# SSD decay exponents from running sums, spread over partitions by DMA and raised on ScalarE, in a bidirectional SSD, S5 and FFN network

## The chip, the cores and the metric

One core of one Trainium2 chip runs the whole network as one program. The metric is the device time of that program in microseconds (us); lower is better.

## The reference, cut to what matters

Two layers on x (512 positions, 1024 channels, float32): an SSD mixer in layer 0 and an S5 mixer in layer 1, each followed by a convolutional FFN and a gated embedding. Only the SSD mixer is touched. It has 32 heads of 64 channels in 4 groups, two directions, and chunks of 128 positions:

```python
def ssd_chunked_scan(xh, dt, a, bm, cm):
    xd = xh * dt                                    # per chunk of 128
    a_cs = jnp.cumsum(dt * a, axis=-1)
    decay_in = jnp.exp(segsum(ad))                  # exp(a_cs[l] - a_cs[s]), l >= s, else 0
    cb = jnp.einsum('bclgn,bcsgn->bgcls', cc, bc)
    y_diag = jnp.einsum('bgcls,bgrcls,bcsgrp->bclgrp', cb, decay_in, xd)
    ...
    y_off = jnp.einsum('bclgn,bcgrpn,bgrcl->bclgrp', cc, carried, jnp.exp(a_cs))
    return y_diag + y_off
y = ssd(xh, dt[0]) + flip(ssd(flip(xh), flip(dt[1]))) + xh * d_skip
y = rms_group(y * silu(z)) * norm_w
return y @ w_out
```

## The kernel before, in words

Every large product has float32 operands split into a rounded part and a remainder. Weights come in units of 128x1024: SP loads a unit into one of two w_raw buffers, ScalarE rounds it (`hi`, line 848), VectorE subtracts (`lo`, line 1193), TensorE runs three products for each tile (`product`, lines 1799 to 1801). `hi(u)` waits until the product of unit u-2 is done, SP's load of u until `lo(u-2)` is done. The two buffers of each kind make this chain strict, and the units are taken in one order everywhere. Each engine runs its own hand-written list of instructions and is held only by semaphore waits; an instruction behind a waiting one waits too.

The SSD mixer (lines 1854 to 1961 on TensorE, 1290 to 1483 on VectorE, 915 to 999 on ScalarE) works through the groups g = 0 to 3. A group takes three pairs of units for x, B and C (product, conv taps on VectorE, silu on ScalarE), the first half of z, transposes of x and B, the product C times B (`cb`), the second half of z, six chunk states (line 1926) with their carry on VectorE (lines 1403 to 1431), six carried outputs (line 1932, scaled on VectorE, lines 1448 and 1452, into yo), and then a loop over four pairs of heads, hp = 0 to 3; n = 4g + hp numbers the 16 pairs. In groups 1 to 3 the four output products of the group before (`out_product`, units w to w+3) are laid between: the first among the states, the others one ahead of each pair's output. The units w+4 and w+5 are the first of what follows. Only one VectorE step after another frees pe_y, so `outputs(hp)` waits for `finish(hp-1)`.

For one pair of heads before the change: ScalarE multiplies the triangular masks by the log decay of each position, 16 times 128x128 (`masked_logs`, line 908, into rr). TensorE sums them with 4 float32 products of 128x512 (`exponents`, lines 1870 and 1871, into pe_e). ScalarE raises 128x1024 of them at once (line 970, into mm). VectorE makes dt times masks for both directions and adds them (`weights`, lines 1357 and 1359, into wf), and multiplies mm by cb and by wf (`weigh`, lines 1365 and 1368). TensorE transposes yo into pe_y by products with the unit matrix (line 1943) and adds the pair's output to it (line 1948). VectorE adds the skip and multiplies by silu(z) (`finish`, lines 1373 and 1377). Loop order on TensorE:

```python
for hp in range(GT):
    if hp + 1 < GT and g:
        out_product(g - 1, hp + 1)
    outputs(hp)
    if hp + 2 < GT:
        exponents(hp + 2)
```

On ScalarE decays(2) and decays(3) stand ahead of the rounding of w+3 and of w+4. On VectorE the order of hp is weigh(hp), lo(w+hp+2), finish(hp-1), weights(hp+1), take_out (line 1333). After the loop the group's variance, root, reciprocal and normalisation follow while TensorE has two units of the next group.

## Time and profile before

| | us |
|---|---|
| three runs, median (lowest to highest) | 1866.92 (1865.04 to 1867.5) |
| the profiled execution, its own time | 1867.26 |
| its span in the trace | 1865.5 |
| TensorE busy | 1635.2 (88%) |
| VectorE busy | 1304.9 (70%) |
| ScalarE busy | 718.4 (39%) |

The span is the time from the first to the last instruction of the trace; the execution's own time is 1.76 us longer. A matmul on float32 gives two records, a transpose one. A record's end is modelled, and successive records overlap.

### The profile page before, as it was taken

The page shows a single profiled execution, that of the slowest core. Times are in us where ns is not written, and L with a number is a line of the kernel's source. Part 1 is how long each engine was busy: PE and PEld are TensorE (multiplying, and loading weights), DVE is VectorE, ACT ScalarE, POOL GpSimd, SP SyncE. Part 2 cuts the span into 40 slices and gives each one's busy share as a digit, 9 for nine tenths or more (in the row PEclk, how much of TensorE's full clock was granted, in tenths as well). Part 3 has the DMA queues.
Part 4 walks back from the last instruction along what each step waited for, and adds up shares of the span by engine and source line. Part 5 has one row for each costly group of instructions (what it writes and reads, how often), then busy time and mean ns, then how long its engine had stood idle before and what let it go on. Part 6 is the DMA issues. An engine that isn't in the chain of part 4 may idle for free.

```text
span 1865.5 us, 20894 instructions
## 1 busy us (share of the span) xinstructions
PE 1635.2 (88%) x7451; PEld 1298.1 (70%) x7451; DVE 1304.9 (70%) x1683; ACT 718.4 (39%) x1079; POOL 163.7 (9%) x200
## 2 busy tenths in 40 slices
PE   3986998998997879989998976878799999999996
PEld 1753766766765668878886755878686888888875
DVE  4587777776776667787769898999365776763355
ACT  3453452452452355532442332220234555542232
POOL 1151000000000180000001120000010000000100
PEclk7997998998998889999999986765799999999998
DMA  2320221211211342343343655652122223333231
GB/s 70 89 59 0 57 67 35 68 57 34 74 51 34 64 105 90 101 138 122 99 142 134 221 191 161 177 154 64 57 91 79 95 96 101 90 107 95 92 94 65
DMA packets 185174, 173.66 MB, mean 93 GB/s; under 512 B 47294, under 2 KB 177934, under 8 KB 181006
## 3 DMA queue, kind: packets, MB, share of 16 engines
q1 hardware_dynamic: 164494, 170.61, 29.4%
q10 hardware_dynamic: 20608, 2.10, 0.9%
q8 instruction: 44, 0.72, 0.2%
q14 instruction: 28, 0.23, 0.0%
HBM read 148.50 MB, written 24.18 MB: 93 GB/s over the span
## 4 chain that ended last, share of the span: by engine, by line
PE 65%; DVE 22%; issue 5%; ACT 4%; SPq 2%; DMA 1%; ACTq 1%; DVEq 0%
PE ring L1799 18%; PE ring L1800 18%; PE ring L1801 18%; DVE w_lo L1193 2%; PE pe_e L1870 2%; PE pe_e L1871 2%; PE pe_y L1948 1%; DVE rb L1601 1%; ACT rr L908 1%; DVE ul L1207 1%; PE ring L1932 1%; PE ring L1926 1%; PE pe_y L1943 1%; DVE cc L1312 1%; PE pe_s L2049 1%
## 5 line engine op out<-in xcount | busy, mean ns | idle before, releaser
L848 ACT ACTIVATE w_hi<-w_raw 128x1024 fp32r<-128x1024 f32 (+1 forms) x233 | 240.0, 1030 | 666.1 <-PE ring L1801 632.9
L1799 PE MATMUL ring<-uh,w_hi 128*128 128x512 f32 (+1 forms) x1160 | 461.3, 398 | 38.4 <-DVE w_lo L1193 32.0
L1800 PE MATMUL ring<-ul,w_hi 128*128 128x512 f32 (+1 forms) x1160 | 455.3, 393 | 0.0
L1801 PE MATMUL ring<-uh,w_lo 128*128 128x512 f32 (+1 forms) x1160 | 454.8, 392 | 0.0
L1193 DVE TENSOR_TENSOR w_lo<-w_raw,w_hi 128x1024 fp32r<-128x1024 f32 (+1 forms) x233 | 279.3, 1201 | 200.5 <-ACT w_hi L848 200.3
L1799 PEld LDWEIGHTS ring<-uh,w_hi 128*128 128x128 f32 (+1 forms) x1160 | 219.7, 189 | 96.7 <-DVE w_lo L1193 26.0
L1800 PEld LDWEIGHTS ring<-ul,w_hi 128*128 128x128 f32 (+1 forms) x1160 | 219.7, 189 | 47.3 <-issue 2.1
L1801 PEld LDWEIGHTS ring<-uh,w_lo 128*128 128x128 f32 (+1 forms) x1160 | 219.5, 189 | 47.1 <-issue 0.6
L1799 PE MATMUL ring<-gh,w_hi 128*128 128x512 f32 x480 | 190.8, 397 | 29.1 <-DVE w_lo L1193 16.0
L1800 PE MATMUL ring<-gl,w_hi 128*128 128x512 f32 x480 | 189.5, 395 | 0.0
L1801 PE MATMUL ring<-gh,w_lo 128*128 128x512 f32 x480 | 189.1, 394 | 0.0
L1692 DVE TENSOR_TENSOR cin<-ring,rstd 128x512 f32<-128x512 f32 x88 | 56.7, 687 | 113.9 <-PE ring L1801 113.9
L1799 PEld LDWEIGHTS ring<-gh,w_hi 128*128 128x128 f32 x480 | 91.7, 191 | 51.7 <-DVE w_lo L1193 19.0
L1702 DVE SCALAR_TENSOR_TENSOR cc<-cin,par,cc 128x512 f32<-128x512 f32 x176 | 123.5, 765 | 0.0
L1801 PEld LDWEIGHTS ring<-gh,w_lo 128*128 128x128 f32 x480 | 91.7, 191 | 19.6
L1800 PEld LDWEIGHTS ring<-gl,w_hi 128*128 128x128 f32 x480 | 91.8, 191 | 18.8
L660 POOL TENSOR_TENSOR var<-sq 128x512 f32<-128x512 f32 x7 | 9.8, 1399 | 796.2 <-ACT sq L864 728.9
L908 ACT ACTIVATE rr<-tri,ad_seq 128x128 f32<-128x128 f32 x256 | 76.4, 388 | 0.0
L1128 ACT ACTIVATE cc<-cin,par 128x512 f32<-128x512 f32 x88 | 66.9, 808 | 1.6 <-DVE cin L1692 1.5
L1312 DVE SCALAR_TENSOR_TENSOR cc<-cin,par,cc 128x512 f32<-128x512 f32 x96 | 65.2, 751 | 2.0 <-ACT cc L937 2.0
L1799 PE MATMUL ring<-yh,w_hi 128*128 128x512 f32 x128 | 55.0, 429 | 10.0 <-DVE yl L1482 10.0
L1207 DVE SCALAR_TENSOR_TENSOR ul<-h,par,uh 128x512 fp32r<-128x512 f32 x40 | 50.2, 1272 | 14.8 <-ACT uh L868 14.6
(249 smaller groups left out, 2206.0 us busy)
## 6 DMA issues: line engine op xcount, KB each, us to landing
w_raw<-in_ffn_w_up SPq DMA_DIRECT2D x88, 512.0 KB, 3.5
w_raw<-in_ffn_w_down SPq DMA_DIRECT2D x40, 512.0 KB, 3.5
w_raw<-in_ssd_w_in SPq DMA_DIRECT2D x32, 512.0 KB, 3.7
s_tables<-tab SPq DMA_DIRECT2D x16, 1024.0 KB, 6.1
slot<-s_tables SPq DMA_DIRECT2D x16, 1024.0 KB, 8.7
w_raw<-in_ssd_w_out SPq DMA_DIRECT2D x16, 512.0 KB, 3.5
w_raw<-in_ple_w_gate SPq DMA_DIRECT2D x16, 512.0 KB, 3.5
w_raw<-in_s_w_glu SPq DMA_DIRECT2D x16, 512.0 KB, 3.4
```

The lines of the kernel that those rows point to most:

```text
L848: act.activation(w_hi[u % 2][:, 0:n], w_raw[:, u % 2, 0:n], ACT.Copy).then_inc(hi_done, 1)
L908: act.activation(rr[:, d, k, c, :], m[:], ACT.Copy, scale=ad_seq[:, c, at:at + 1]).then_inc(r_done, 1)
L1128: act.activation(cc[:, 2 * half + j, :], cin[:, j, 1:1 + SEQ], ACT.Identity, scale=dcol(i * 2 + (C_FCW + c)), bias=dcol(i * 2 + (C_FCB + 2 ...
L1193: dve.tensor_tensor(w_lo[u % 2][:, 0:n], w_raw[:, u % 2, 0:n], w_hi[u % 2][:, 0:n].bitcast(F32), ALU.subtract).then_inc(lo_done, 1)
L1207: dve.scalar_tensor_tensor(out=ul[:, m, :], in0=h[:, m, :], scalar=col(NORM_COL[r] + m), in1=uh[:, m, :].bitcast(F32), op0=ALU.mult, op1=A ...
L1312: dve.scalar_tensor_tensor(out=cc[:, q % 4, :], in0=cin[:, j, tap:tap + SEQ], scalar=col(C_CONVW + tap * CONV_T + chans[j]), in1=cc[:, q % ...
L1692: dve.tensor_tensor(cin[:, j, 2:2 + SEQ], bank(t + 2 * half + j), rstd[:], ALU.mult).then_inc(evac, 1)
L1702: dve.scalar_tensor_tensor(out=cc[:, 2 * half + j, :], in0=cin[:, j, 1 + tap:1 + tap + SEQ], scalar=dcol(i * 2 + (C_FCW + c)), in1=cc[:, 2 ...
L1799: pe.matmul(o, wh[:, k, c], rh[:, k0 + k, :], start=first and k == 0, stop=False)
L1800: pe.matmul(o, wh[:, k, c], rl[:, k0 + k, :], start=False, stop=False)
L1801: mm_ = pe.matmul(o, wl[:, k, c], rh[:, k0 + k, :], start=False, stop=last and k == nk - 1)
L1870: pe.matmul(pe_e[:, k, :], gt[:], rr[:, 0, k].rearrange("p c l -> p (c l)"), start=True, stop=False)
```

## The change

The running sums cs of the log decays are made once, as rows (one partition for a head and direction) and as columns (one partition for a position). The rows go to DRAM. For each pair SP loads a 128x2048 block in which every partition has the same four rows (two directions, two heads), 1 MB into one of three buffers, `rows_`, of which a buffer is free after the output of three pairs before. ScalarE then does max(cs[s] - cs[l], 0) in place, 16 times 128x128, and exp(ln(dt) - that) in place, 16 times 128x128. The masks are multiplied into cb, once for each group and direction. VectorE multiplies each direction by its cb and adds the two. The carried part is transposed into pe_e (transposes, not products with the unit matrix), for the next pair ahead of this pair's output, and is added to the skip by `add_yoff`; `finish` adds the pair's output. masked_logs, exponents and weights are gone. SP's list has the row loads among the weight loads.

```diff
         ad_seq = sb("ad_seq", [P, SB, 2 * HEADS], where=ssd)
...
         yl = sb("yl", [P, GT, SEQ], F32R, ssd)
-        dtT = mm[0:2 * HEADS, 0, 0, :]
...
                     load(U[("out", g)] + i, rows(A["ssd_w_out"][0], GT * g, GT, 256 * i, 256))
 
+            def row_load(n):
+                sp.wait_ge(cs_saved, 16)
+                if n >= 3:
+                    sp.wait_ge(y_full, n - 2)
+                src = bass.AP(tensor=cs_dram.tensor, offset=2 * n * SEQ, ap=[[0, P], [HEADS * SEQ, 2], [1, 2 * SEQ]])
+                sp.dma_start(rows_[n % 3][:].rearrange("p d k l -> p d (k l)"), src).then_inc(row_in[n % 3], 16)
+
             for g in range(GROUPS):
-                ssd_loads(g)
-                if g:
+                if g == 0:
+                    xbc_loads(0, 0, 6)
+                    z_loads(0)
+                    xbc_loads(1, 0, 2)
+                    sp.wait_ge(cs_evac, 1)
+                    sp.dma_start(cs_dram, cs_row).then_inc(cs_saved, 16)
+                    for n in range(GT + 2):
+                        row_load(n)
+                else:
+                    xbc_loads(g, 2, 6)
+                    row_load(GT * g + 2)
+                    z_loads(g)
                     out_loads(g - 1)
+                    row_load(GT * g + 3)
+                    if g + 1 < GROUPS:
+                        for n in range(2):
+                            xbc_loads(g + 1, n, n + 1)
+                            row_load(GT * g + GT + n)
             out_loads(GROUPS - 1)
 
...
                 act.activation(adT, spw, ACT.Ln).then_inc(dtx, 1)
 
             def dt_sums():
+                act.wait_ge(cs_full, 1)
+                act.activation(cs_row, pe_e[0:2 * HEADS, 0, :], ACT.Copy).then_inc(cs_evac, 1)
                 act.wait_ge(evac, T["sums"] + 1)
                 act.activation(epq[:], epq[:], ACT.Exp).then_inc(e_done, 1)
                 act.wait_ge(evac, T["totals"] + 1)
                 act.activation(etot[:], etot[:], ACT.Exp).then_inc(e_done, 1)
-
-            def masked_logs(n):
-
-                if n >= 1:
-                    act.wait_ge(e_full, n)
-                for d, m in ((0, le), (1, ge)):
-                    for k in range(2):
-                        for c in range(SB):
-                            at = HEADS * d + 2 * n + k
-                            act.activation(rr[:, d, k, c, :], m[:], ACT.Copy, scale=ad_seq[:, c, at:at + 1]
-                                           ).then_inc(r_done, 1)
+                act.wait_ge(ln_in, 1)
+                act.activation(dt_ln[:], dt_seq[:], ACT.Ln).then_inc(ln_done, 1)
 
             def vec(dst, src, f, scale=1.0):
...
-                        if g:
-                            masked_logs(GT * g)
-                        else:
+                        if g == 0:
                             dt_steps()
                         hi_to(z + 5)
...
@@ -957,19 +979,28 @@
                         act.activation(zs[:, 2 * i + j, :], zs[:, 2 * i + j, :], ACT.Silu).then_inc(z_silu, 1)
                 if g == 0:
                     dt_sums()
-                    act.wait_ge(adt, 2)
-                    act.wait_ge(evac, T["seq"] + 1)
-                    masked_logs(0)
 
 
                 def decays(hp):
                     n = GT * g + hp
-                    act.wait_ge(e_full, n + 1)
-                    if n >= 2:
-                        act.wait_ge(y_full, n - 1)
-                    act.activation(mm[:, n % 2, :, :], pe_e[:], ACT.Exp).then_inc(exp_done, 1)
-                    if hp + 1 < GT:
-                        masked_logs(n + 1)
+                    act.wait_ge(row_in[n % 3], 16 * (n // 3) + 16)
+                    for d in range(2):
+                        for k in range(2):
+                            at = HEADS * d + 2 * n + k
+                            for c in range(SB):
+                                row = rows_[n % 3][:, d, k, c * P:(c + 1) * P]
+                                act.activation(row, row, ACT.Relu, scale=-1.0, bias=cs_seq[:, c, at:at + 1]
+                                               ).then_inc(fall_done, 1)
+                    for d in range(2):
+                        act.wait_ge(fall_done, 16 * n + 8 * d + 8)
+                        if n == 0:
+                            act.wait_ge(ln_done, 1)
+                        for k in range(2):
+                            at = HEADS * d + 2 * n + k
+                            for c in range(SB):
+                                row = rows_[n % 3][:, d, k, c * P:(c + 1) * P]
+                                act.activation(row, row, ACT.Exp, scale=-1.0, bias=dt_ln[:, c, at:at + 1]
+                                               ).then_inc(exp_done, 1)
...
-                dve.tensor_copy(epq[:], bank(T["sums"]).rearrange("p (a c h) -> p a c h", a=2, c=SB)).then_inc(evac, 1)
+                s_t = bank(T["sums"]).rearrange("p (a c h) -> p a c h", a=2, c=SB)
+                dve.tensor_copy(epq[:], s_t)
+                dve.wait_ge(cs_full, 1)
                 dve.wait_ge(filled, FILL["totals"] + 1)
+                dve.tensor_copy(cs_seq[:], s_t[:, 0]).then_inc(evac, 1)
                 dve.tensor_copy(etot[:], bank(T["totals"])[:, 0:SB * 2 * HEADS].rearrange("p (c h) -> p c h", c=SB)
                                 ).then_inc(evac, 1)
...
+                dve.wait_ge(eq_done, 1)
+                dve.tensor_scalar(dt_seq[:], dt_seq[:], 1e-38, None, ALU.max).then_inc(ln_in, 1)
...
-
-                def spread(ap, hp, d):
-                    h0 = HEADS * d + HPG * g + 2 * hp
-                    return ap[:, :, h0:h0 + 2].rearrange("p c h -> p h c").unsqueeze(3).to_broadcast([P, 2, SB, P])
-
-                def mask(ap):
-                    return ap[:].unsqueeze(1).unsqueeze(1).to_broadcast([P, 2, SB, P])
-
-                def weights(hp):
-                    n = GT * g + hp
-                    if n >= 1:
-                        dve.wait_ge(m_done, n)
-                    for dst, d, m in ((wf, 0, le), (wb, 1, ge)):
-                        dve.tensor_tensor(dst[:], spread(dt_seq, hp, d), mask(m), ALU.mult).then_inc(w_done, 1)
-                    dve.wait_ge(w_done, 3 * n + 2)
-                    dve.tensor_tensor(wf[:], wf[:], wb[:], ALU.add).then_inc(w_done, 1)
+                dve.wait_ge(filled, FILL[("cb", g)] + 1)
+                cb_ = bank(T[("cb", g)]).rearrange("p (c l) -> p c l", c=SB)
+                for d, m in ((0, le), (1, ge)):
+                    cb_op = dve.tensor_tensor(cb_mask[d].rearrange("p (c l) -> p c l", c=SB), cb_, m[:].unsqueeze(1).to_broadcast([P, SB, P]), ALU.mult)
+                    cb_op.then_inc(*((cb_low, 1) if d == 0 else (evac, 1)))
 
                 def weigh(hp):
                     n = GT * g + hp
-                    m = mm[:, n % 2]
-                    dve.wait_ge(exp_done, n + 1)
-                    dve.tensor_tensor(m, m, cbT[:].unsqueeze(1).to_broadcast([P, 2, SEQ]), ALU.mult).then_inc(m_half, 1)
-                    dve.wait_ge(m_half, n + 1)
-                    dve.wait_ge(w_done, 3 * n + 3)
-                    dve.tensor_tensor(m, m, wf[:].rearrange("p h c l -> p h (c l)"), ALU.mult).then_inc(m_done, 1)
+                    if hp == 0:
+                        dve.wait_ge(cb_low, g + 1)
+                        dve.wait_ge(evac, T[("cb", g)] + 1)
+                    e = rows_[n % 3]
+                    for d in range(2):
+                        dve.wait_ge(exp_done, 16 * n + 8 * d + 8)
+                        cb_ = cb_mask[d].unsqueeze(1).to_broadcast([P, 2, SEQ])
+                        dve.tensor_tensor(e[:, d], e[:, d], cb_, ALU.mult).then_inc(m_half, 1)
+                    dve.wait_ge(m_half, 2 * n + 2)
+                    dve.tensor_tensor(e[:, 0], e[:, 0], e[:, 1], ALU.add).then_inc(m_done, 1)
+
+                def add_yoff(hp):
+                    n = GT * g + hp
+                    dve.wait_ge(yt_full, n + 1)
+                    dve.scalar_tensor_tensor(out=xT[:, hp, :], in0=xT[:, hp, :], scalar=d_col[:, n:n + 1],
+                                             in1=pe_e[:, n % 2, :], op0=ALU.mult, op1=ALU.add).then_inc(y_pre, 1)
 
                 def finish(hp):
                     n = GT * g + hp
                     dve.wait_ge(y_full, n + 1)
-                    dve.scalar_tensor_tensor(out=xT[:, hp, :], in0=xT[:, hp, :], scalar=d_col[:, n:n + 1],
-                                             in1=pe_y[:], op0=ALU.mult, op1=ALU.add).then_inc(y_skip, 1)
+                    dve.wait_ge(y_pre, n + 1)
+                    dve.tensor_tensor(xT[:, hp, :], xT[:, hp, :], pe_y[:], ALU.add).then_inc(y_skip, 1)
...
@@ -1410,7 +1444,6 @@
                 decay_x(0)
                 decay_x(1)
                 if g:
-                    weights(0)
...
-                if g == 0:
-                    weights(0)
                 for hp in range(GT):
                     weigh(hp)
                     if g:
                         lo_to(w + hp + 2)
+                    add_yoff(hp)
                     if hp:
                         finish(hp - 1)
-                    if hp + 1 < GT:
-                        weights(hp + 1)
-                        if g:
-                            take_out(g - 1, hp + 1)
+                    if hp + 1 < GT and g:
+                        take_out(g - 1, hp + 1)
                 finish(GT - 1)
...
+                for d, m in ((0, le), (1, ge)):
+                    for c in range(SB):
+                        mm_ = pe.matmul(pe_e[HEADS * d:HEADS * d + HEADS, 0, c * P:(c + 1) * P],
+                                        ad_seq[:, c, HEADS * d:HEADS * d + HEADS], m[:], start=True, stop=True)
+                mm_.then_inc(cs_full, 1)
...
@@ -1859,18 +1894,6 @@
                     pe.matmul(pe_s[:], ones[:], var[:], start=True, stop=False).then_inc(gsq_used, 1)
                     pe.wait_ge(gsq, GT * g + GT)
                     pe.matmul(pe_s[:], ones[:], sq[:, 1, :], start=False, stop=True).then_inc(gsq_used, 1)
-
-                def exponents(hp):
-
-                    n = GT * g + hp
-                    pe.wait_ge(r_done, 16 * n + 16)
-                    if n:
-                        pe.wait_ge(exp_done, n)
-                    for k in range(2):
-                        pe.matmul(pe_e[:, k, :], gt[:], rr[:, 0, k].rearrange("p c l -> p (c l)"), start=True, stop=False)
-                        mm_ = pe.matmul(pe_e[:, k, :], lt[:], rr[:, 1, k].rearrange("p c l -> p (c l)"), start=False,
-                                        stop=True)
-                    mm_.then_inc(e_full, 1)
...
-                if g:
-                    exponents(0)
-                else:
+                if g == 0:
...
-                    if n == 4:
-                        if g:
-                            pe.wait_ge(yl_done, GT * g)
-                            out_product(g - 1, 0)
-                        else:
-                            exponents(0)
+                    if n == 4 and g:
+                        pe.wait_ge(yl_done, GT * g)
+                        out_product(g - 1, 0)
...
-                exponents(1)
...
+                def transposes(hp):
+                    n = GT * g + hp
+                    if hp == 0:
+                        pe.wait_ge(evac, T[("yoff", g)] + 6)
+                        pe.wait_ge(yo_add, 2 * g + 2)
+                        if n == 0:
+                            pe.wait_ge(cs_evac, 1)
+                    if n >= 2:
+                        pe.wait_ge(y_pre, n - 1)
+                    for c in range(SB):
+                        mm_ = pe.transpose(pe_e[:, n % 2, c * P:(c + 1) * P], yo[:, c, hp * P:(hp + 1) * P], eye[:])
+                    mm_.then_inc(yt_full, 1)
+
                 def outputs(hp):
                     n = GT * g + hp
                     if n:
                         pe.wait_ge(y_skip, n)
-                    if hp == 0:
-                        pe.wait_ge(evac, T[("yoff", g)] + 6)
-                        pe.wait_ge(yo_add, 2 * g + 2)
...
                     for k in range(2):
                         for c in range(SB):
                             mm_ = pe.matmul(pe_y[64 * k:64 * k + 64, c * P:(c + 1) * P],
                                             xseq[:, c, (2 * hp + k) * HD:(2 * hp + k + 1) * HD],
-                                            mm[:, n % 2, k, c * P:(c + 1) * P], start=False,
-                                            stop=True, skip_group_check=True)
+                                            rows_[n % 3][:, 0, k, c * P:(c + 1) * P], start=True,
+                                            stop=True)
                     mm_.then_inc(y_full, 1)
 
+                transposes(0)
                 for hp in range(GT):
                     if hp + 1 < GT and g:
                         out_product(g - 1, hp + 1)
+                    if hp + 1 < GT:
+                        transposes(hp + 1)
                     outputs(hp)
-                    if hp + 2 < GT:
-                        exponents(hp + 2)
                     if hp:
```

## Rows read from the trace of the kernel before

**Rows 1.** The page, part 4: who holds the chain that ended last.

```profile
PE 65%; DVE 22%; issue 5%; ACT 4%; SPq 2%; DMA 1%; ACTq 1%; DVEq 0%
```

**Rows 2.** Windows: start:end, length, busy time (instructions) of each engine, clock, DMA share, GB/s.

```profile
345.40:481.80 136.40, 122.75 (x522) 90.00 (x521) 100.48 (x126) 56.37 (x110) 3.34 (x2) 0.96 0.19 54
626.00:1865.50 1239.50, 1120.18 (x5333) 928.01 (x5331) 869.63 (x1147) 465.25 (x599) 99.56 (x82) 0.92 0.37 114
```

**Rows 3.** Groups by line and form, group 2 (345.4 to 481.8): busy us, mean ns.

```profile
L908 ACT ACTIVATE rr<-tri,ad_seq 128x128 f32<-128x128 f32 x64 | 19.1, 390 | 0.0
...
L1870 PE MATMUL pe_e<-rr,tri 128*128 128x512 f32 x16 | 8.4, 605 | 0.0
...
L1871 PE MATMUL pe_e<-rr,tri 128*128 128x512 f32 x16 | 8.2, 592 | 0.0
...
L1943 PE MATMUL pe_y<-eye,yo 128*128 128x128 f32 x32 | 6.2, 356 | 8.9 <-DVE xT L1373 8.9
...
L1357 DVE TENSOR_TENSOR wf<-dt_seq,tri 128x1024 f32<-128x1024 f32 x4 | 4.9, 1222 | 0.0
...
L1373 DVE SCALAR_TENSOR_TENSOR xT<-xT,d_col,pe_y 128x512 f32<-128x512 f32 x4 | 3.0, 743 | 4.3 <-PE pe_y L1948 4.3
...
L1896 PE MATMUL ring<-eye,xT 128*128 128x128 f32 x16 | 2.2, 279 | 0.0
```

**Rows 4.** Timeline of VectorE, group 2: start, length, line, operation, idle before.

```profile
392.55 1.29 DVE L1324 TENSOR_TENSOR zs<-ring,rstd 128x512 f32<-128x512 f32 x2 [5.42 <-PE ring L1801]
393.75 2.35 DVE L1193 TENSOR_TENSOR w_lo<-w_raw,w_hi 128x1024 fp32r<-128x1024 f32 x2
396.84 0.69 DVE L1222 COPY car<-ring 128x512 f32<-128x512 f32 x1 [0.73 <-PE ring L1926]
...
417.82 1.22 DVE L1365 TENSOR_TENSOR mm<-mm,cbT 128x1024 f32<-128x1024 f32 x1
...
434.57 1.23 DVE L1193 TENSOR_TENSOR w_lo<-w_raw,w_hi 128x1024 fp32r<-128x1024 f32 x1 [7.04 <-ACT w_hi L848]
```

**Rows 5.** Timeline of ScalarE, group 2.

```profile
394.72 1.28 ACT L970 ACT_TABLE_LOAD   x1
...
406.10 1.06 ACT L848 ACTIVATE w_hi<-w_raw 128x1024 fp32r<-128x1024 f32 x1 [4.38 <-PE ring L1801]
...
428.82 4.78 ACT L908 ACTIVATE rr<-tri,ad_seq 128x128 f32<-128x128 f32 x16
```

**Rows 6.** Timeline of TensorE, group 2.

```profile
410.99 5.31 PE L1932 MATMUL ring<-car,cT 128*128 128x512 f32 x12
...
460.02 2.88 PE L1948 MATMUL pe_y<-mm,xseq 128*64 128x128 f32 x16
```

**Rows 7.** Windows around a stall of TensorE in group 2; granted clock third from the end.

```profile
433.00:436.50 3.50, 0.33 (x2) 0.00 (x0) 1.89 (x3) 1.54 (x4) 0.00 (x0) 1.00 0.00 0
436.50:438.00 1.50, 1.49 (x7) 1.49 (x8) 1.50 (x2) 0.00 (x0) 0.00 (x0) 0.53 0.54 109
438.00:444.00 6.00, 6.00 (x28) 3.92 (x27) 5.93 (x7) 0.00 (x0) 0.00 (x0) 0.83 0.18 63
```

**Rows 8.** Timeline of SP's DMA issues, group 2: 49.21 us from first to last.

```profile
408.49 49.21 SPq L425 DMA_DIRECT2D w_raw<-in_ssd_w_in  x4
```

**Rows 9.** DMA: one lone 1 MB read at 1064, and the tile's sixteen, issue to landing.

```profile
slot<-s_tables SPq DMA_DIRECT2D x1, 1024.0 KB, 5.7
...
DMA to landing us min/median/max: 4.8/8.7/12.8
```

**Rows 10.** Group 0: timeline of VectorE, and (last row) the chain that ended last.

```profile
127.39 1.42 DVE L1403 TENSOR_TENSOR xd<-xseq,epq 128x512 f32<-128x512 f32 x2
...
138.09 0.69 DVE L1431 TENSOR_TENSOR car<-ytmp,ring 128x512 f32<-128x512 f32 x1 [1.18 <-PE ring L1926]
...
154.96 1.22 DVE L1357 TENSOR_TENSOR wf<-dt_seq,tri 128x1024 f32<-128x1024 f32 x1
...
187.98 2.81 PE pe_y L1948 x16
```

55 lines of the change are left out of this document (30 added, 25 removed).

## The prediction

> **What bounds the kernel now.** I read the chain that ended last first [rows 1]: TensorE holds 65% of the span, VectorE 22%, ScalarE 4%. An average over the program doesn't price an edit in one stage, so I took the windows next [rows 2]. The change lies between 41.7 and 626; the 1239.5 us behind keep their work and only start earlier. Groups 1, 2 and 3 of the SSD mixer repeat one pattern of about 136 us; I work it out on group 2, in which TensorE is busy 122.75 us of 136.4, VectorE 100.5, ScalarE 56.4. So TensorE is nearly full on average. The groups by line [rows 3] say what each removed and added operation costs, and the timelines [rows 4 to 6, 8] say which wait ends last. There the reader is to see that the loop over head pairs is not TensorE's alone: VectorE's subtraction for unit w+3 comes at 434.57 after 7.04 us of waiting for ScalarE's rounding [rows 4], which stands behind exponents and 16 masked logs (428.82 and 4.78 us) [rows 5], and `outputs(1)` waits for `finish(0)` behind it. TensorE sits still from 433.0 to 436.5 [rows 7]. The loop's last output ends at 460.02 + 2.88 = 462.9 [rows 6]; the next group's product starts there.
>
> **The change part by part.** *TensorE loses* four products of 128x512 for each pair. They are 16 + 16 records a group with 8.4 + 8.2 us busy [rows 3], but records overlap: twelve like them take 5.31 us, (5.31 - 0.59) / 11 = 0.43 from start to start [rows 6]. So 8 records cost 3.4 us a pair, 55 us over 16 pairs. Transposes by unit matrix, 8 records of 6.2 / 32 = 0.19 us a pair, become 4 true transposes of 2.2 / 16 = 0.14 [rows 3], 1.0 us less. *VectorE loses* three operations of 1.22 us a pair and gains one such and an add of 512 elements, bounded by its like, 0.74 us [rows 3]: 1.7 us less a pair. A second masked cb costs 0.7 us a group, in a stretch where VectorE waits 5.42 us for the second half of z, of which 3.7 more are now free [rows 4]: nothing. *ScalarE loses* 16 activations and one big exponential and gains 32 small ones. Sixteen took 4.78 us at 0.39 each [rows 3, 5], so (4.78 - 0.39) / 15 = 0.293 from start to start; 32 take 31 x 0.293 + 0.39 = 9.5 us, where the old pair took 4.8 + 1.0. Bounds: 0.293 if the start rate holds in place with a bias, 0.39 if each waits for the one before (12.5 us). I take 0.293, the row of the same shape with one operand per partition. *SP gains* 16 row loads of 1 MB, and these are waits: the load for hp = 3 waits for `outputs(0)` of its own group, and the weights of w+4 stand behind it, those of w+5 behind a wait for `outputs(1)`, and w+6 behind one for `outputs(2)`. Before, these issues were spread over 49.21 us with nothing ahead of them but VectorE's release [rows 8]. A row load reads the same 8 KB of DRAM for 128 partitions; no row shows such a read. The loads for hp = 0, 1 and 2 are issued tens of microseconds before their use, so they cost nothing while landing stays under some 20 us; w+5 is issued near 434 and rounded at 442, w+6 near 448 and not before the root at 463, with 1 MB ahead of each. The nearest rows are 1 MB reads: 5.7 us alone, 4.8 to 12.8 in all, 8.7 the median [rows 9]. SP issues it alone, so I take 5.7; the ends stay for the range.
>
> The Trainium skill, "DMA: Bandwidth & Descriptors", section Bandwidth, has 6.15 us for 1 MB issued by GpSimd; with it the gain below would be about 2 us less. The trace's lone 5.7 is used.
>
> *Group 2, step by step, on the old clock.* (1) The second half of z ends as before. Two subtractions from 393.75 now hold VectorE until 396.1, where exponents held the first state until 396.84 [rows 4]: 0.7 us gained out of the 3.4 removed, no more, since VectorE is late next. (2) ScalarE has z's silu done at 394.7 and a table load to 396.0, as before [rows 5]; decays(0) ends 405.5, just as `out_product(0)` ends (406.10 - 0.7), so rounding w+2 moves by those 0.7. (3) exponents(1) is gone, so the carried outputs start at once and VectorE scales them from 410.5 on: `weigh(0)` starts 416.3 for 417.82 [rows 4], 1.5 gained. (4) The last carried output needs the bank of the second, scaled by about 412, and ends at 412.9. TensorE now waits for all of yo, since the transposes stand ahead of `out_product(1)`, where before the product followed the carried outputs at once [rows 6] and VectorE scaled beside it: 3.4 us of idleness. Such a gap was followed by a clock of 0.53 for 1.5 us and 0.83 for 6 [rows 7], half rate for 1.5 + 2.0 us, 1.7 us of work lost. So: transposes to 416.9, product to 422.4, cold start to 424.1, next transposes and `outputs(0)` (0.6 + 1.5) to 426.2. (5) decays(1) and (2) end 416.0 and 425.5, rounding w+3 ends 426.5. ScalarE now waits for hp = 3's rows: 426.2 + 5.7 = 431.9, ends decays(3) 441.4, rounds w+4 by 442.4. (6) VectorE had `weigh(2)` done at about 437 and waits for that; subtraction 1.2, add_yoff 0.7, `finish(1)` releases pe_y 0.8 later, 445.1. (7) `outputs(2)` runs cold (2.9, the same row as the old last output [rows 6]); VectorE has the rest of finish, take_out and weigh(3) (0.6 + 1.2 + 3.7), subtraction, add_yoff, finish(2) (1.2 + 0.7 + 0.8), 453.3; `outputs(3)` cold to 456.2. That is 462.9 - 456.2 = 6.7 us less. Behind it the group's variance, root and normalisation follow as they did. Groups 1 and 3 alike: 20 us. Of the 15 to 18 us that TensorE loses a group, more than half becomes idleness, first behind ScalarE.
>
> *Group 0* has no output products. Sums as rows are 8 small products more, 16 records of 128 columns at 0.18 us cold (2.88 / 16 [rows 6]), 2.9 us, and the copies that xd waits for go behind them with a table and clamp: xd moves from 127.39 to about 132.3. Without exponents (1.18 us of waiting at 138.09) and the masked logs behind them, which put `weights(0)` at 154.96 [rows 10], the carried outputs are scaled by about 150 and weigh(0) starts there. Rows: sums 128, copy, a small store bounded by 1 and 5.7 us (taken 2.5, since a lone 1 MB takes 5.7), rows landed about 137.5, decays(0) with exp's table 148.3. From here ScalarE is the pace: four times 9.5, 176.6; the last multiply and add 2.5, `outputs(3)` cold 2.9: 182 against 187.98 + 2.81 = 190.8 [rows 10]. Gain 8 to 9, taken as 8, because three row loads are in flight together at the start.
>
> *Sum.* 3 x 6.7 + 8 = 28 us. The profiled execution took 1867.3 (span 1865.5 + 1.8), 0.3 above the median shown, so 1867.3 - 28 = 1839.3, and 1839 as a median.
>
> **The rivals.**
>
> *Rows come quickly, the clock holds* (chance 0.2). If a load lands in 4.8 us [rows 9] and the 3.4 us gap isn't followed by half rate, each group gains 0.9 + 1.7 more: 28 + 8 = 36, 1831. For: the load is alone on the queues. Against: the gap of [rows 7] was as long.
>
> *Every removed product comes off* (0.05): TensorE as the only bound, 55 + 16 = 71 us less at most, some 61 with the new products and transposes, 1806. For: 65% of the chain. Against: VectorE's and ScalarE's steps of (1), (3) and (5).
>
> *Rows are late; slower than before* (0.06 past the line, 0.03 on it, 0.08 short of it, 1852 to 1863). Place: ScalarE at decays(3), behind SP's wait and a landing time L. Nothing hides it: w+4 and finish(1) queue behind. Each microsecond of L beyond 5.7 costs one in each of groups 1 to 3 and one at the start of group 0: 28 - 4 (L - 5.7), zero at L = 12.7, the longest 1 MB landing in the trace [rows 9]. At twice the median, 17.4 us (128 readers of the same 8 KB), 28 - 47: 1886. For: that read is of a kind never shown. Against: 5.7 alone.
>
> *The clock stays down* (0.03). With exponents gone TensorE's work from 394 on is bursts. If all four output products ran at 1.2 GHz, 11 us for 5.5, and pairs in turn, I get the last output at 471 for 462.9: 3 x 8.5 - 8, 1885. Against: after its gap the clock was back at 1.0 within some 3.5 us of half rate [rows 7]. This is also what the Trainium skill, "TensorE: Matmul & The Clock Gate", section HAM oscillation, warns of: an engine that waits between bursts starts every burst cold. By that rule the removed products were worth something as filling; the trace agrees for single gaps (clock 0.53 behind one).
>
> *ScalarE in place is slower* (0.03): at 0.39 from start to start decays take 12.5 us. Decays(0) to (3) then run without a gap to 448.1, and w+4 is rounded at 449.2 for 442.4: 6.8 us a group, and 4 x 3 in group 0. 28 - 20 - 12 = -4, 1871. Against: the rows of the same shape [rows 5].
>
> **How the numbers follow.** The forecast, 1839, has 0.52, with a range of its own from 1832 to 1850: L from 4.8 to 8.7 is 4 less or 12 more, and a second clock gap, among the states, where TensorE now waits for VectorE, would be 1.7 more a group. Rows early 0.2, all comes off 0.05, late but faster 0.08: faster 0.85. On the line 0.03. Late 0.06, clock 0.03, ScalarE 0.03: slower 0.12. The range leaves out the all-comes-off case, the line and the slower ones, 2 in 10: from 1824, which is the early case with `outputs(2)` and `(3)` warm in three groups (1.4 each, 8 in all) to 1862. A measurement of this kernel can tell about 0.2%, 3.7 us, from no change.
>
> **What would show it.** Right: TensorE busy in a group near 108 to 111 us of about 129.7; decays(3) waiting some 6 us for the row load; VectorE's subtraction for w+4, not w+3, with the long wait on ScalarE; 32 activations in 9.5 us; loads landing in 5 to 7; clock near 0.5 at the start of out_product(1). Wrong: a landing over 9 us, small activations further apart than 0.3, or a group whose wait for ScalarE is gone, so that TensorE's relief shows in full.

## The result and the profile after

The changed kernel takes 1836.68 us (median of 4 runs, 1833.54 to 1837.47) beside 1866.74 (4 runs, 1865.04 to 1867.5) of the kernel before: ratio 0.984, 95% interval [0.982, 0.986]. That is 30 us less where 28 were forecast. The profiled execution took 1833.54, its span 1831.8.

Busy time by engine and the shares of the chain that ended last, kernel after:

```profile
PE 1578.1 (86%) x7275; PEld 1269.4 (69%) x7275; DVE 1282.2 (70%) x1673; ACT 781.0 (43%) x1323; POOL 165.6 (9%) x200
...
PE 59%; DVE 25%; ACT 9%; issue 4%; DMA 2%; ACTq 1%; SPq 1%; DVEq 0%
```

TensorE lost 57 us of busy time, 1635.2 to 1578.1, and the execution only some 30 of them: its share of the chain fell from 65% [rows 1] to 59%, ScalarE's rose from 4% to 9%, and the DMAs' from 1% to 2%. The windows of the same stretches, a whole group 2 and everything behind the mixer:

```profile
331.50:461.10 129.60, 107.90 (x473) 81.68 (x473) 94.38 (x122) 71.11 (x170) 2.53 (x2) 0.93 0.30 90
598.40:1831.80 1233.40, 1122.60 (x5333) 930.15 (x5332) 870.50 (x1147) 465.08 (x599) 99.66 (x82) 0.92 0.37 114
```

In a group TensorE is busy 14.9 us less than in [rows 2] and the group is 6.8 shorter, so 8.1 of it became idle time, and the clock granted over the group fell from 0.96 to 0.93. Where the time went can be read at VectorE's first step of the variance, which stands behind each group's last output. Its rows in group 0 and in group 3, of the kernel before:

```profile
198.25 0.69 DVE L1470 TENSOR_SCALAR var<-pe_s 128x512 f32<-128x512 f32 x1 [5.95 <-PE pe_s L1861]
602.71 0.69 DVE L1470 TENSOR_SCALAR var<-pe_s 128x512 f32<-128x512 f32 x1 [1.88 <-PE pe_s L1861]
```

The same in the changed kernel:

```profile
190.84 0.69 DVE L1500 TENSOR_SCALAR var<-pe_s 128x512 f32<-128x512 f32 x1 [6.37 <-PE pe_s L1896]
575.11 0.69 DVE L1500 TENSOR_SCALAR var<-pe_s 128x512 f32<-128x512 f32 x1 [1.88 <-PE pe_s L1896]
```

Group 0 gave 7.4 us and the three groups behind it (602.71 - 198.25) - (575.11 - 190.84) = 20.2, together 27.6. The span is shorter by 33.7. The other 6.1 lie behind the mixer, in work that the change doesn't touch, 5.0 of them between two operations of GpSimd (the kernel before, then the changed one):

```profile
1111.26 0.95 POOL L822 MEMSET bqm<- 128x1024 f32 x1 [6.03 <-PE pe_e L2137]
1354.05 1.29 POOL L660 TENSOR_TENSOR var<-sq 128x512 f32<-128x512 f32 x1 [67.33 <-issue]
```

```profile
1083.44 0.95 POOL L853 MEMSET bqm<- 128x1024 f32 x1 [6.03 <-PE pe_e L2162]
1321.21 1.30 POOL L691 TENSOR_TENSOR var<-sq 128x512 f32<-128x512 f32 x1 [65.61 <-issue]
```

That is 242.8 us before and 237.8 after, and it is 239.2 to 240.7 in the eleven experiments. Part of the 5.0 is a spread from one execution to another: the profiled execution of the changed kernel was the fastest of its four, 3.1 us under their median. But all twelve traces with the changed mixer lie under the one of the kernel before. From group 3's variance to the end they take 1256.7 to 1260.2 us, the kernel before 1262.8. The medians differ by 30.1, so some 2.5 us come from work behind the mixer that wasn't edited, and why is not known.

ScalarE in group 2:

```profile
411.03 1.04 ACT L879 ACTIVATE w_hi<-w_raw 128x1024 fp32r<-128x1024 f32 x1
417.61 4.79 ACT L992 ACTIVATE rows<-rows,ad_seq 128x128 f32<-128x128 f32 x16 [5.54 <-DMA rows<-log_decays]
...
426.98 1.04 ACT L879 ACTIVATE w_hi<-w_raw 128x1024 fp32r<-128x1024 f32 x1
```

This is the step on which the forecast rested: 32 activations take 9.4 us (417.61 to 426.98), and before them ScalarE stands 5.54 us because the rows of decays(3) haven't landed, and the rounding of w+4 comes behind it. SP's issue for them, the chain's piece, and the median of all sixteen row loads:

```profile
411.68 0.37 SPq L499 DMA_DIRECT2D rows<-log_decays  x1
...
411.68 5.90 DMA rows<-log_decays
...
rows<-log_decays SPq DMA_DIRECT2D x16, 1024.0 KB, 5.9
```

The load is issued when `outputs(0)` ends (second row below, 410.02 + 1.58), and lands 5.9 us later. VectorE passes the wait on, and TensorE's last two outputs wait for VectorE. TensorE's rows, with the first transposes on top, and then VectorE's, of which the first two are used further down:

```profile
401.94 0.78 PE L1962 MATMUL pe_e<-eye,yo 128*128 128x128 f32 x4 [2.53 <-DVE yo L1481]
...
410.02 1.58 PE L1972 MATMUL pe_y<-rows,xseq 128*64 128x128 f32 x16
...
430.59 2.88 PE L1972 MATMUL pe_y<-rows,xseq 128*64 128x128 f32 x16 [5.22 <-DVE xT L1408]
439.19 2.88 PE L1972 MATMUL pe_y<-rows,xseq 128*64 128x128 f32 x16 [5.72 <-DVE xT L1408]
```

```profile
391.17 1.29 DVE L1369 TENSOR_TENSOR h<-h,ring 128x512 f32<-128x512 f32 x2 [2.84 <-PE ring L1831]
...
401.80 1.22 DVE L1394 TENSOR_TENSOR rows<-rows,cb_fwd 128x1024 f32<-128x1024 f32 x1
...
428.06 1.23 DVE L1224 TENSOR_TENSOR w_lo<-w_raw,w_hi 128x1024 fp32r<-128x1024 f32 x1 [5.70 <-ACT w_hi L879]
```

The long wait for ScalarE's rounding is now that of w+4 (5.70 us) and no longer that of w+3 (7.04 [rows 4]). Windows of the stall ahead of the first transposes and of what follows (the third number from the end is the granted clock):

```profile
399.00:402.70 3.70, 1.17 (x6) 0.77 (x6) 3.56 (x6) 3.70 (x14) 0.00 (x0) 0.95 0.01 2
402.70:404.00 1.30, 1.30 (x5) 1.01 (x4) 1.30 (x2) 1.30 (x5) 0.00 (x0) 0.50 0.00 0
404.00:410.00 6.00, 6.00 (x25) 4.74 (x24) 2.34 (x4) 6.00 (x22) 0.00 (x0) 0.86 0.00 0
```

TensorE stands 2.53 us, and `out_product(1)` starts at a granted clock of 0.50, the 1.2 GHz level.

### The profile page after: what moved, and what is told of

Read it like the earlier page. It is cut to its first block, busy times and chain, and to the rows that moved or that the text cites. A ratio compares the mean times of both kernels' runs of the same rounds, so it can differ in the third digit from the quotient of the medians.

```text
span 1831.8 us, 20798 instructions
## 1 busy us (share of the span) xinstructions
PE 1578.1 (86%) x7275; PEld 1269.4 (69%) x7275; DVE 1282.2 (70%) x1673; ACT 781.0 (43%) x1323; POOL 165.6 (9%) x200
## 4 chain that ended last, share of the span: by engine, by line
PE 59%; DVE 25%; ACT 9%; issue 4%; DMA 2%; ACTq 1%; SPq 1%; DVEq 0%
PE ring L1829 19%; PE ring L1830 18%; PE ring L1831 18%; ACT rows L992 3%; ACT rows L1002 3%; DVE w_lo L1224 2%; DVE rb L1631 2%; DMA rows<-log_decays 1%; DVE ul L1238 1%; PE pe_y L1972 1%; DVE cc L1348 1%; DVE s_prod L1590 1%; DVE tab L1551 1%; DVE ytmp L1502 1%; DVE rstd L1247 1%
## 5 line engine op out<-in xcount | busy, mean ns | idle before, releaser
L1829 PE MATMUL ring<-uh,w_hi 128*128 128x512 f32 (+1 forms) x1160 | 461.9, 398 | 36.5 <-DVE w_lo L1224 30.1
L1732 DVE SCALAR_TENSOR_TENSOR cc<-cin,par,cc 128x512 f32<-128x512 f32 x176 | 125.2, 774 | 0.0
L992 ACT ACTIVATE rows<-rows,ad_seq 128x128 f32<-128x128 f32 x256 | 76.4, 387 | 20.1 <-DMA rows<-log_decays 20.1
L1972 PE MATMUL pe_y<-rows,xseq 128*64 128x128 f32 x256 | 38.3, 372 | 52.1 <-DVE xT L1408 49.7
L1002 ACT ACTIVATE rows<-rows,dt_seq 128x128 f32<-128x128 f32 x256 | 76.4, 387 | 0.0
L1972 PEld LDWEIGHTS pe_y<-rows,xseq 128*64 128x64 f32 x256 | 32.9, 191 | 56.4 <-DVE xT L1408 52.6
```

Source lines behind the costliest of these rows:

```text
L992: act.activation(row, row, ACT.Relu, scale=-1.0, bias=cs_seq[:, c, at:at + 1]).then_inc(fall_done, 1)
L1002: act.activation(row, row, ACT.Exp, scale=-1.0, bias=dt_ln[:, c, at:at + 1]).then_inc(exp_done, 1)
L1732: dve.scalar_tensor_tensor(out=cc[:, 2 * half + j, :], in0=cin[:, j, 1 + tap:1 + tap + SEQ], scalar=dcol(i * 2 + (C_FCW + c)), in1=cc[:, 2 ...
L1829: pe.matmul(o, wh[:, k, c], rh[:, k0 + k, :], start=first and k == 0, stop=False)
L1972: mm_ = pe.matmul(pe_y[64 * k:64 * k + 64, c * P:(c + 1) * P], xseq[:, c, (2 * hp + k) * HD:(2 * hp + k + 1) * HD], rows_[n % 3][:, 0, k, ...
```

## The experiments

All edits are made in the changed kernel. A time "behind z" is counted from VectorE's eviction of the second half of z in the same group, so that groups and kernels compare. Each run stands beside runs of the kernel before: 1866.53 us for the first four, 1865.49 for the next four, 1866.59 for the last three.

**A fourth row buffer.** Rows for hp = 3 go into the memory of the carried state, which is free once TensorE has read it for the carried outputs, and every hp has a buffer of its own.

```diff
-                if n >= 3:
-                    sp.wait_ge(y_full, n - 2)
+                if n % 4 == 3:
+                    sp.wait_ge(filled, FILL[("yoff", n // 4)] + 6)
+                elif n >= 4:
+                    sp.wait_ge(y_full, n - 3)
...
-                sp.dma_start(rows_[n % 3]...
+                sp.dma_start(row_buf[n % 4]...
```

> The changed kernel with one edit: the rows of the last head pair of each group (hp = 3) go to a fourth buffer (the carried states' memory, read out by then), so their load waits for the carried outputs and no longer for outputs(0). My theory: in groups 1 to 3 ScalarE's wait for these rows (5.5 us in group 2) was in front of unit w+4's rounding and so of all that ends the group. ScalarE then goes straight on: each of groups 1 to 3 shorter by 5.0 us, group 0 unchanged, 1836.7 - 15 = 1822. Rival A: VectorE or TensorE was as late anyway: under 1.5 us a group, over 1832. Rival B: landing time does not matter at all, the gap behind the carried outputs does: 1836 to 1837.

Measured 1823.05 us, ratio 0.977 [0.975, 0.978]: 13.6 us off the changed kernel. Timelines of SP and of ScalarE in group 2:

```profile
397.73 0.37 SPq L503 DMA_DIRECT2D car<-log_decays  x1
...
410.17 4.20 ACT L996 ACTIVATE car<-car,ad_seq 128x128 f32<-128x128 f32 x14
```

The load is issued 12.4 us before decays(3), which starts without a wait, and the group takes 126.3 us for 129.7. By the variance the three groups are 10.5 us shorter together, where 15 were expected; the rest of the 13.6 isn't in them. In this trace the low clock followed both stalls of TensorE in every group, and `outputs(0)` ended 1.0 us later than in the changed kernel, so the wait for the rows was worth more than these 10.5. The row load behind SP's wait held the end of the group, as step (5) had it.

**Later rows.** SP reads an extra 1 MB of rows into idle memory just ahead of the load for hp = 3, in three groups.

```diff
                     out_loads(g - 1)
+                    sp.wait_ge(y_full, GT * g + 1)
...
+                    sp.dma_start(car[:]..., first).then_inc(spare_in, 16)
                     row_load(GT * g + 3)
```

> The changed kernel with one extra 1 MB read of the same kind just ahead of the row load of hp = 3 in groups 1 to 3, into spare memory; it is not used. The row load lands later by what the extra read takes, 3 to 5.5 us. My theory: each microsecond of landing costs one in each of groups 1 to 3: 1836.7 + 9 to 16 = 1846 to 1853. Rival: something else is as late as the rows, or the reads overlap fully: under 1840.

Measured 1847.34, ratio 0.990 [0.989, 0.992], 10.7 us more. The chain's piece and ScalarE, group 2:

```profile
416.69 8.94 DMA rows<-log_decays
...
425.66 4.79 ACT L997 ACTIVATE rows<-rows,ad_seq 128x128 f32<-128x128 f32 x16 [7.47 <-DMA rows<-log_decays]
```

Landing went from 5.90 to 8.94 us, with the issue 0.46 behind the extra one. Over groups 1, 2 and 3 decays(3) starts 4.9, 3.4 and 3.7 us later behind z than in the changed kernel, and the last output ends 4.9, 3.4 and 3.7 us later. One microsecond of landing costs one of the group: the price by which the rival "rows are late" was worked out.

**The output product ahead of the first transposes.** TensorE has `out_product(1)` to do while VectorE scales the carried outputs.

```diff
-                transposes(0)
+                if g == 0:
+                    transposes(0)
                 for hp in range(GT):
                     if hp + 1 < GT and g:
                         out_product(g - 1, hp + 1)
+                        if hp == 0:
+                            transposes(0)
```

> The changed kernel with one edit: in groups 1 to 3 the first transposes of the carried y stand behind out_product(1) on TensorE, not ahead of it. My theory: the wait for yo (3.7 us idle at 399.0 to 402.7 in group 2, then 1.3 us at clock 0.50 and 6 at 0.86) delays outputs(0), and outputs(0) delays the row load of hp = 3. outputs(0) comes 4.5 to 5 us earlier, the load too, ScalarE's wait falls from 5.5 to about 1 us: 4.2 us a group, 1836.7 - 12.6 = 1824. Rival A (only the row load's own place matters, the gap is covered): under 1 us a group. Rival B: outputs(0) then waits for weigh(0), and the row lands no earlier than before: 1836.

Measured 1828.34, ratio 0.980 [0.978, 0.983]: 8.3 us less where 12.6 were expected. In group 2 `outputs(0)` starts at 28.1 behind z for 31.5, 3.4 earlier where 4.5 to 5 had been expected, and ScalarE's wait for the rows falls from 5.54 to 1.71:

```profile
411.57 4.79 ACT L992 ACTIVATE rows<-rows,ad_seq 128x128 f32<-128x128 f32 x16 [1.71 <-DMA rows<-log_decays]
```

The last output ends at 59.7 for 63.5, 3.8 earlier, just as much as decays(3) starts earlier; by the variance the groups are 2.4, 3.5 and 3.4 us shorter, 9.3 in all. So the stall of step (4) is a cost of the order in which the transposed part is carried, not of the transposes.

**Filling a stall.** Four products on idle operands of ones and masks, whose result nothing reads, in groups 1 to 3: once ahead of the first transposes (`e3`, the diff below), once ahead of the chunk states, where exponents(0) had stood (`e4`).

```diff
+                if g:
+                    pe.wait_ge(y_pre, GT * g)
+                    for i in range(4):
+                        pe.matmul(pe_e[:, 0, :], ones[:], tri[:]..., start=True, stop=True)
```

> The changed kernel with four extra float32 products of 128x512 on constants in the gap ahead of the first transposes of groups 1 to 3; their result is overwritten and is not part of the computation. It adds 3.4 us of TensorE work where TensorE waits 3.4 to 3.7 us. My theory of the clock: the half-rate stretch behind the gap (1.7 us of lost work) goes, outputs(0), the row load and the group's end come 1.3 to 1.7 us earlier: 1836.7 - 4 to 5 = 1832. Rival A: the clock does not depend on this gap, nothing changes: 1836 to 1837. Rival B: the extra products overrun the gap and cost: up to 1840.

> The changed kernel with four extra float32 products of 128x512 on constants put back where exponents(0) stood in groups 1 to 3, between the second half of z and the chunk states; their result is not used. My theory: VectorE's two subtractions end 0.7 us ahead of where the old products held the states, so 3.4 us of TensorE work cost only 0.7 us a group there: 1836.7 + 2 = 1839. Rival A: TensorE is the bound, all 3.4 us show in each group: 1847. Rival B: the products keep the clock up later on and nothing is lost: 1836.

Measured 1839.59, ratio 0.987 [0.985, 0.990], and 1835.72, ratio 0.984 [0.982, 0.985]: no gain from either. A window of `e3` over the end of the filled stall and what follows, group 2:

```profile
400.00:410.00 10.00, 10.00 (x41) 6.75 (x40) 7.09 (x10) 10.00 (x36) 0.00 (x0) 1.00 0.00 1
```

The clock did hold at 1.00 where it had fallen to 0.50. But the filling ran about 0.8 us past the moment at which VectorE was ready (403.70 for 402.90), and in this trace the earlier stall, among the states, was followed by the low clock in all three groups: `out_product(0)` ends 14.3 to 15.2 us behind z, where it ends at 12.64 in groups 2 and 3 of the changed kernel. `e4` fills that earlier stall: `out_product(0)` ends at 13.5 in every group, 0.8 later than where the clock had held and 0.8 earlier than in group 1 of the changed kernel, where it hadn't. Behind the second stall, which `e4` leaves, the clock fell in group 2 alone. Neither filling gave back more than it cost.

**Both that helped.**

> The fourth buffer of e1 and the order of e2 together. My theory: both take away the same wait of ScalarE for the rows of hp = 3. With it gone ScalarE's chain of four decays and three roundings (decays(3) at 34.4 us after the second half of z in e1, without a gap before it) holds unit w+4, whatever TensorE does ahead of it: 0 to 1 us a group less than e1, 1820 to 1823. Rival A: the gains add (5 and 3.8 us a group): 1812. Rival B: TensorE alone was the bound behind e1 (its outputs were 7.6 us apart), so its earlier start of 4.4 us a group shows in full: 1810.

Measured 1821.08, ratio 0.976 [0.974, 0.977]. The two are worth 13.6 and 8.3 us alone and 15.6 together. In group 2 the last output ends 4.4 and 3.8 us earlier behind z with one of them and 5.6 with both. With both, VectorE waits 2.38 us for the rounding of w+4 behind decays(3), and TensorE waits for VectorE:

```profile
420.13 1.22 DVE L1228 TENSOR_TENSOR w_lo<-w_raw,w_hi 128x1024 fp32r<-128x1024 f32 x1 [2.38 <-ACT w_hi L883]
...
431.27 2.88 PE L1976 MATMUL pe_y<-car,xseq 128*64 128x128 f32 x16 [7.02 <-DVE xT L1412]
```

**The rounding ahead of decays(3)**, in the changed kernel alone.

```diff
                     if hp + 2 < GT:
+                        if hp == 1 and g:
+                            hi_to(w + hp + 3)
                         decays(hp + 2)
```

> The changed kernel with one edit on ScalarE: in groups 1 to 3 the rounding of unit w+4 stands ahead of decays(3), not behind it. It needs out_product(2), which ends about 0.5 us ahead of the rows' landing, so it fits in ScalarE's wait. My theory: the long way was decays(3), rounding w+4, subtraction, finish(1), outputs(2), finish(2), outputs(3); without decays(3) at its head outputs(2) comes some 5.5 us earlier and outputs(3) then waits for weigh(3): 6 us a group, 1836.7 - 18 = 1819. Rival A: the end waits for decays(3) and weigh(3) in any case: under 2 us a group, over 1831. Rival B: decays(3) starts later behind the rounding and this eats the gain: 1835.

Measured 1826.6, ratio 0.979 [0.977, 0.981]: 10 us less where 18 were expected. decays(3) now starts behind the rounding, 41.0 us behind z for 39.1, and the subtraction that follows weigh(3) takes 2.28 us for 1.22, beside one of GpSimd's sums. ScalarE's rounding names its own weights, which SP issues behind the row load:

```profile
414.86 1.06 ACT L879 ACTIVATE w_hi<-w_raw 128x1024 fp32r<-128x1024 f32 x1 [6.49 <-DMA w_raw<-in_ssd_w_in]
```

From this I took it that the weights behind the row load were the cause of the miss, worth 6 us. To test it, SP issues w+4 ahead of that load:

```diff
+                    if g + 1 < GROUPS:
+                        xbc_loads(g + 1, 0, 1)
                     row_load(GT * g + 3)
```

> e6_rounding_ahead with one more edit: SP issues the load of w+4 ahead of the row load for hp = 3, which waits for outputs(0). Theory A (e6_rounding_ahead gave 10 us and not 18 because its rounding waited 6.5 us for its weights behind that row load): the load is issued when its buffer is free, near 392, the rounding runs while ScalarE waits for the rows, decays(3) starts at 39.1 after the second half of z as in the changed kernel and not at 41.0, outputs(3) near 54.6 for 56.5: 1826.6 - 6 = 1821, and 1819 if weigh(3) is no longer split. Theory B (the late start had another cause): 1826.

Measured 1827.13, ratio 0.979 [0.977, 0.980]: nothing. My reading of `e6` fell; SP and ScalarE in group 2:

```profile
391.61 0.37 SPq L431 DMA_DIRECT2D w_raw<-in_ssd_w_in  x1
...
415.30 1.06 ACT L882 ACTIVATE w_hi<-w_raw 128x1024 fp32r<-128x1024 f32 x1 [5.37 <-PE ring L1836]
```

The load is issued 17 us earlier, and the rounding starts where it did, 39.9 us behind z for 40.0: it now waits for TensorE. The rounded copy has two buffers, and w+4's is that of w+2, in use until `out_product(2)` ends. In `e6` that product ended 38.8 us behind z and the weights landed at 40.0, so the releaser named there was the later of two by 1.3 us, and no more than that could be won. In `e11` the product ended at 39.8, since the low clock had followed the stall among the states, which took most of it back. Group 3 isn't reached by the edit: there w+4 is a unit of the last output product, whose load still stands behind the row load.

**The transposition undone.** The carried part is again added to pe_y by products with the unit matrix, just ahead of the pair's output, and `finish` again adds the skip and the output in one operation.

```diff
-                        mm_ = pe.transpose(pe_e[:, n % 2, ...], yo[:, c, hp * P:(hp + 1) * P], eye[:])
+                        pe.matmul(pe_y[:, c * P:(c + 1) * P], yo[:, c, hp * P:(hp + 1) * P], eye[:], start=c == 0, ...)
...
-                    add_yoff(hp)
...
+                    transposes(hp)
                     pe.wait_ge(m_done, n + 1)
```

> One part of the change undone: the carried y goes into pe_y by products with the unit matrix ahead of each pair's output, as before, and finish adds skip and output in one operation; transposes and add_yoff are gone. Decays, rows and masks stay as changed. My theory: the transposition part cost time where it was put, since it made TensorE wait for yo ahead of out_product(1); undone, outputs(0) comes 4.6 us earlier, the row load with it, and each later output pays 0.9 warm or 2.1 cold for the products: 4 us a group less, 1824 to 1826. Rival A: transposes and the split add saved time (0.05 us against 0.19, and an add off the way to pe_y): 1838 to 1842.

Measured 1833.47, ratio 0.982 [0.981, 0.984], 3 us under the changed kernel and not the 11 to 13 expected. The intervals of the two overlap; in the traces group 3's variance comes 2.6 us earlier. So this part of the change, as it is placed, cost about 3 us. Against `e2`, whose TensorE also has the product first, it is 5.1 us slower: the transposes with their own add are worth about 5 us, their place cost 8. These are rough, since the clock behind the stall among the states differs between the traces (`out_product(0)` ends 0.4 and 1.6 us later than in `e2` in groups 1 and 3).

**Three edits together**, fourth buffer, product first, rounding ahead; and the same with `finish(2)` ahead of weigh(3) on VectorE:

```diff
+                    if hp == GT - 1:
+                        finish(hp - 1)
                     weigh(hp)
...
-                    if hp:
+                    if hp and hp < GT - 1:
                         finish(hp - 1)
```

> The fourth row buffer and the output product first (the two edits of e5_both), and ScalarE's rounding of w+4 ahead of decays(3) as in e6_rounding_ahead. With the fourth buffer the load of w+4 is issued at 397.59 in e5_both, so the rounding has its weights at 409.69. Theory A (after e5_both VectorE's 2.38 us of waiting for that rounding are still on the path to outputs(3), and the miss of e6_rounding_ahead was the load standing behind the row load): rounding w+4 409.7 to 410.7, decays(3) to 420.1, subtraction straight behind weigh(2) at 417.8, outputs(2) at 420.2 for 422.67, weigh(3) to 426.5, outputs(3) at 429.1 for 431.27: 2.2 us less in each of three groups, 1821 - 6.6 = 1814. Theory B (another wait is already as late: ScalarE's decays(3) or the closing of the group): 1821.

> e9_three_edits, and for the last pair of a group VectorE's add and gate of the pair before (finish(2)) stands ahead of weigh(3) instead of behind weigh(3), the subtraction for w+5 and add_yoff(3). Theory A (outputs(3) waits for VectorE's queue and for nothing else, of which the subtraction and add_yoff, 1.2 + 0.7 less overlap, now lie behind it): outputs(3) some 1.1 us earlier than in e9_three_edits, 3 us in all, 1811. Theory B (ScalarE's last exponents or the product TensorE has in hand come last): no change from e9_three_edits.

Measured 1815.12, ratio 0.973 [0.972, 0.975], and 1813.7, ratio 0.972 [0.970, 0.973]. Both are faster than either kernel; between them the intervals overlap. The traces say where the second differs, on the chain that ends group 0 (`e9`, then `e10`):

```profile
178.47 0.73 DVE xT L1407
179.20 0.61 DVE xT L1414
...
179.85 2.88 PE pe_y L1978 x16
```

```profile
175.86 2.18 DVE car L1402
...
178.17 2.85 PE pe_y L1980 x16
```

The skip's add and `finish` (0.73 and 0.61) are gone from the chain, and the last output of group 0 starts 61.2 us behind z for 62.3, the 1.1 expected. (Group 0 ends 1.7 us earlier, but 0.6 of this was there at z, ahead of the edit.) In groups 1 to 3 nothing came: the last output starts 54.4 us behind z for 54.3. There weigh(3) starts 1.3 later, behind `finish(2)`, and two of its three operations take nearly twice their time, where in `e9` one did. VectorE and GpSimd in `e10`, group 2:

```profile
419.25 2.28 DVE L1400 TENSOR_TENSOR car<-car,bT 128x1024 f32<-128x1024 f32 x1
421.56 2.17 DVE L1402 TENSOR_TENSOR car<-car 128x1024 f32<-128x1024 f32 x1
...
419.00 1.45 POOL L704 TENSOR_TENSOR var<-sq 128x512 f32<-128x512 f32 x1 [119.23 <-ACT sq L1027]
421.25 1.40 POOL L707 TENSOR_TENSOR var<-var,sq 128x512 f32<-128x512 f32 x1 [0.80 <-ACT sq L1027]
```

`finish(2)` ended earlier, so GpSimd's second sum of squares came 4.0 us earlier behind z, onto weigh(3), where the first stood already. That these sums lengthen VectorE's operations rests on the rows standing side by side (last section); no run moved the sums.

## Why the prediction was right

In group 2 the second half of z stands at 392.55 before and at 378.53 after, so 14.02 us are added to the new rows to lay them on the steps of the forecast.

- Steps (1) and (2), `out_product(0)` ends at 405.4 (406.10 - 0.7): 391.17 + 14.02 = 405.2.
- Step (3), weigh(0) at 416.3: 415.8.
- Step (4), a stall of 3.4 us and a clock of half rate behind it, `outputs(0)` ends at 426.2: the stall was 2.5, the clock 0.50 and then 0.86, the end 411.60 + 14.02 = 425.6. The Trainium skill ("TensorE: Matmul & The Clock Gate", section HAM oscillation) says that a TensorE that waits between bursts of products starts the next burst at the low clock. Groups 2 and 3 agree for this stall, group 1 doesn't. There the low clock followed the stall among the states (last section), and behind the same stall ahead of the transposes, 2.52 us, the clock stayed at 1.00:

```profile
270.50:273.60 3.10, 0.94 (x3) 0.12 (x1) 2.96 (x5) 3.10 (x12) 0.00 (x0) 1.00 0.00 0
273.60:275.00 1.40, 1.03 (x7) 0.94 (x8) 1.40 (x3) 1.40 (x6) 0.00 (x0) 1.00 0.00 0
```

So each group paid for one low clock ahead of `outputs(0)`, as the forecast had it, but in group 1 at another place. That it came out at one and not at none or two is luck: `e4` has two groups with none, and every group of `e1` has two.

- Step (5), rows landed 431.9, w+4 rounded 442.4: 431.6 and 442.0. The load took 5.9 us where 5.7, the lone 1 MB read, had been taken [rows 9]. The Trainium skill's figure for 1 MB issued by GpSimd, 6.15 us ("DMA: Bandwidth & Descriptors", section Bandwidth), would have been as near.
- Steps (6) and (7), `outputs(3)` ends at 456.2: 439.19 + 2.88 + 14.02 = 456.1. Forecast 6.7 us less a group, measured 20.2 / 3 = 6.7. TensorE's busy time in the group, forecast at 108 to 111, is 107.9.
- Group 0, forecast 8, measured 7.4. Two terms were off and nearly cancelled. The sums and the copies were quicker: the first rows landed at 136.4 and not 137.5. The end was dearer: ScalarE's last exponents end at 175.4 for the forecast's 176.6, and I had 2.5 us from there to the last output for VectorE's multiply and add; it took 180.13 - 175.40 = 4.7. Of the 2.2 too little, 1.3 are add_yoff(3) and `finish(2)`, which stand behind weigh(3) and which `e10` takes away, and 0.95 are the add of weigh(3), 2.17 us for 1.22, beside a sum of GpSimd. That these terms nearly cancel is luck.
- The sum. The mixer gave 27.6 us where 28 were forecast. The medians differ by 30.1; the 2.5 between lie behind the mixer, and nothing in the forecast stands for them.

Group 0 after: ScalarE's start, the add of weigh(3), and the chain at its end:

```profile
136.44 4.79 ACT L992 ACTIVATE rows<-rows,ad_seq 128x128 f32<-128x128 f32 x16 [5.20 <-DMA rows<-log_decays]
...
176.65 2.17 DVE L1396 TENSOR_TENSOR rows<-rows 128x1024 f32<-128x1024 f32 x1
...
175.40 1.24 DVE rows L1394
...
178.74 0.74 DVE xT L1401
179.48 0.61 DVE xT L1408
180.13 2.88 PE pe_y L1972 x16
```

Of the rivals, "rows come quickly" failed on both its conditions (5.9 us, and one low clock in each group); "ScalarE in place is slower" on 4.77 us for 16; "the clock stays down" on 0.86 in the 6 us behind the stall; "rows are late" on the landing, while its price of one for one holds. "Everything comes off" has a slip in its sum: the 71 us already have the new transposes in them, so with the 2.9 of the new products it is 68, and 1799 for 1806. It didn't come, but it shows what was missed: with a buffer more and three changes of order the kernel comes to 1813.7, 53 us under the kernel before, so most of TensorE's relief (57 us of busy time) was there, held back by one transfer and three orders. The text of the forecast names what is late next, the row load and the rounding behind it, but not what stands behind that: the buffer of the rounded copy, and VectorE's queue.

Not settled: these 2.5 us, and what decides whether the clock falls behind a stall. Not tried: a third buffer for the rounded weights, and moving GpSimd's sums off weigh(3).

## What to carry to other kernels

When a producer moves from TensorE to a DMA and a small operation, the buffer count decides: look up when the last buffer comes free and what the issuing queue has behind it, since a wait on SP of one landing time becomes a wait of two engines. Cost the last step of a chain by everything that stands in its engine's queue, not by the operation alone. And a releaser named in a trace is the last, not the only one: before removing it, look up when the next would have let go. Where a clock can fall behind a stall or not, compare single groups only where it did the same in both traces.
